# Head of a two-layer encoder kernel: row transfers on ScalarE's queue, the first weight chunk ahead of them, table rows behind the first modulated input

## The reference

```
cond = silu(c)
for i in (0, 1):
    mod = (cond @ mod_w[i] + mod_b[i]).reshape(B, 6, D_MODEL)
    h = modulate(rmsnorm(x, g[0]), mod[:, 0], mod[:, 1])
    y = diff_attention(h, ...)   if i == 0 else   mlstm_layer(h, ...)
    x = x + mod[:, 2][:, None, :] * rmsnorm(y, g[1])
    h = modulate(rmsnorm(x, g[2]), mod[:, 3], mod[:, 4])
    y = swiglu(h, ...)           if i == 0 else   moe_swiglu(h, ...)
    x = x + mod[:, 5][:, None, :] * rmsnorm(y, g[3])
```

## Time and profile before

| what | us |
| --- | --- |
| median of 3 runs | 1612.39 |
| lowest, highest | 1611.19, 1613.15 |
| the profiled execution's own time | 1613.23 |
| span of the profiled execution | 1611.4 |
| TensorE busy in the span | 1493.7 (93%) |
| VectorE busy | 472.5 (29%) |
| ScalarE busy | 161.5 (10%) |
| mean granted clock of TensorE, of full | 0.973 |

### The profile page before, as it was taken

The page is one execution under the profiler, slowest core; times in us unless marked ns, Lnnn a source line. Parts: engine busy times, 40 slices in busy tenths (PEclk is TensorE's granted clock), DMA queues, the critical chain, the costliest instruction groups (busy, mean ns, idle before and its releaser), DMA issues.

```text
span 1611.4 us, 21780 instructions
## 1 busy us (share of the span) xinstructions
PE 1493.7 (93%) x9526; PEld 1091.1 (68%) x9526; DVE 472.5 (29%) x1003; ACT 161.5 (10%) x428; POOL 37.6 (2%) x84
## 2 busy tenths in 40 slices
PE   4997999999999899989999999999898899998997
PEld 3864587885477677443356887778683597886884
DVE  1577327351047455151211111111112311011113
ACT  2005210000020121021000000000000000000000
POOL 1000100000011100010000000000000000000000
PEclk8999999999999999999989999999999999999998
DMA  9996129859432110759998999999999999999995
GB/s 336 387 393 230 57 93 366 320 188 360 156 105 105 53 52 1 274 196 357 401 370 337 392 395 392 395 393 395 393 382 398 389 378 395 392 395 392 395 392 202
DMA packets 205824, 483.49 MB, mean 300 GB/s; under 512 B 4241, under 2 KB 6698, under 8 KB 205714
## 3 DMA queue, kind: packets, MB, share of 16 engines
q1 hardware_dynamic: 205106, 481.46, 79.9%
q10 hardware_dynamic: 608, 0.47, 0.1%
HBM read 480.86 MB, written 1.05 MB: 299 GB/s over the span
## 4 chain that ended last, share of the span: by engine, by line
PE 74%; DMA 13%; DVE 5%; SPq 4%; issue 3%; ACT 1%; POOL 0%; DVEq 0%; POOLq 0%
PE ps L1209 18%; PE ps L1729 15%; PE ps L1196 10%; DMA ring<-in_moe_w_gate 7%; PE ps L1787 7%; PE ps L1745 4%; PE ps L1585 3%; DMA ring<-in_moe_w_down 3%; DMA ring<-in_attn_w_in 3%; SPq L620 2%; PE ps L1752 2%; PE ps L1253 2%; PE ps L1635 2%; PE ps L1797 2%; SPq L617 1%
## 5 line engine op out<-in xcount | busy, mean ns | idle before, releaser
L1209 PE MATMUL ps<-hT,ring 128*128 128x256 f32 x1472 | 326.7, 382 | 5.1 <-issue 1.8
L1209 PEld LDWEIGHTS ps<-hT,ring 128*128 128x128 f32 x1472 | 278.6, 191 | 49.0 <-issue 6.5
L1729 PE MATMUL ps<-arena,ring 128*128 128x208 f32 (+1 forms) x1792 | 295.7, 327 | 6.7 <-DMA ring<-in_moe_w_gate 6.7
L1729 PEld LDWEIGHTS ps<-arena,ring 128*128 128x128 f32 x1792 | 292.8, 191 | 9.5 <-DMA ring<-in_moe_w_gate 9.0
L1196 PE MATMUL ps<-ring,arena 128*128 128x512 f32 x368 | 158.8, 592 | 1.3 <-DVE arena L2243 1.3
L1787 PE MATMUL ps<-arena,ring 128*128 128x208 f32 (+1 forms) x896 | 149.3, 327 | 2.6 <-DMA ring<-in_moe_w_down 2.6
L1787 PEld LDWEIGHTS ps<-arena,ring 128*128 128x128 f32 x896 | 145.2, 190 | 3.7 <-DMA ring<-in_moe_w_down 3.0
L1745 PE MATMUL ps<-ring,arena 128*32 128x256 f32 x1792 | 110.2, 401 | 30.6 <-issue 30.6
L1196 PEld LDWEIGHTS ps<-ring,arena 128*128 128x128 f32 x368 | 69.5, 190 | 87.2 <-issue 87.2
L1745 PEld LDWEIGHTS ps<-ring,arena 128*32 128x32 f32 x1792 | 62.7, 116 | 76.2 <-issue 46.1
L2034 DVE SCALAR_TENSOR_TENSOR arena<-ring,cond,arena 128x512 f32<-128x512 f32 x140 | 105.3, 752 | 5.0
(11 more groups left out here) (348 smaller groups left out, 1089.5 us busy)
## 6 DMA issues: line engine op xcount, KB each, us to landing
ring<-in_moe_w_down SPq DMA_DIRECT2D x56, 2048.0 KB, 19.3
ring<-in_moe_w_gate SPq DMA_DIRECT2D x55, 2048.0 KB, 19.4
ring<-in_moe_w_up SPq DMA_DIRECT2D x55, 2048.0 KB, 20.0
ring<-in_mod_w SPq DMA_DIRECT2D x24, 2048.0 KB, 17.0
ring<-in_mlstm_w_in SPq DMA_DIRECT2D x8, 2048.0 KB, 9.1
ring<-in_attn_w_in SPq DMA_DIRECT2D x6, 2048.0 KB, 19.9
ring<-in_ffn_w_gate SPq DMA_DIRECT2D x5, 2048.0 KB, 12.4
ring<-in_ffn_w_up SPq DMA_DIRECT2D x5, 2048.0 KB, 12.8
```

Of the source, the lines that this page charges most:

```text
L1209: ins = pe.matmul(dst, w[:, k, c * P:(c + 1) * P], hT[:, k, :], start=(k == 0), stop=(k == KT - 1))
L1729: ins = pe.matmul(dst, weights_in[:, k, ft * P:(ft + 1) * P], xq[:, k, BASE:BASE + w], start=(k == 0), stop=(k == KT - 1))
```

## The change

- `sp_program`: behind the wait for `rows_clear` and the transfer of `c`, the first chunk of `mod_w` is issued at once, then `x`, then the other chunks.
- ScalarE waits for `rows_clear` at its start and issues the seven other row transfers.
- Lambda's rows and the seven table transfers are issued by ScalarE behind its part of `hT`.
- TensorE: four products of `keep_busy` ahead of each of the three later `mod_product`s, three behind the first `mod_turn`; `turn_tables` behind j = 1 instead of ahead of j = 0; `spread_gates(0)` and `(1)` behind j = 2 and 3 instead of 0 and 1.
- VectorE: lambda's product behind the copies of j = 1, its rest behind those of j = 3; `fold_gates(0)` and `(1)` behind j = 2 and 3.

```diff
         def sp_program(sp):
             sp.wait_ge(rows_clear, 1)
             sp.dma_start(rows[0:8, 1, :], a["c"][0].rearrange("(t p) -> t p", p=P)).then_inc(rows_loaded, 16)
-            sp.dma_start(rows[8:72, 1, :], a["norm_g"]...).then_inc(rows_loaded, 16)
...
-            sp.dma_start(rows[96:112, 0, :], a["mlstm_norm"][0]...).then_inc(rows_loaded, 16)
-            sp.dma_start(x[:], a["x"][0].rearrange("(t p) d -> p t d", p=P)).then_inc(x_loaded, 16)
             for i, (m, f, n, r) in enumerate(PLAN):
...
                 sp.dma_start(dst, weights(m, f, n)).then_inc(landed[i % SLOTS], 16)
+                if i == 0:
+                    sp.dma_start(x[:], a["x"][0].rearrange("(t p) d -> p t d", p=P)).then_inc(x_loaded, 16)
...
         def act_program(act):
-            act.dma_start(lam_in[:], a["attn_lambda"][0]...).then_inc(lam_loaded, 16)
+            act.wait_ge(rows_clear, 1)
+            act.dma_start(rows[8:72, 1, :], a["norm_g"]...).then_inc(rows_loaded, 16)
...
+            act.dma_start(rows[96:112, 0, :], a["mlstm_norm"][0]...).then_inc(rows_loaded, 16)
...
-            for m, name in enumerate(("mlstm_w_q", "mlstm_w_k", "mlstm_w_v")):
...
-            act.dma_start(b_router[:], ...).then_inc(small_loaded, 16)
             act.wait_ge(consts, 1)
             act.wait_ge(u_free, 1)
...
                 ins.then_inc(u_free, 1)
+            act.dma_start(lam_in[:], a["attn_lambda"][0]...).then_inc(lam_loaded, 16)
+            for m, name in enumerate(("mlstm_w_q", "mlstm_w_k", "mlstm_w_v")):
...
+            act.dma_start(b_router[:], ...).then_inc(small_loaded, 16)
             act.wait_ge(tables_turned, 3)
...
             for j in range(1, EARLY):
+                keep_busy(ps[:, 5], 4)
                 mod_product(0, j, j)
             mods = EARLY
             mod_turn(1)
-            turn_tables()
+            keep_busy(ps[:, 5], 3)
...
-                if j < 2:
-                    spread_gates(j)
+                if j == 1:
+                    turn_tables()
+                elif 2 <= j < 4:
+                    spread_gates(j - 2)
                 if j:
                     for m in MODS[0][j - 1]:
...
-            dve.wait_ge(lam_loaded, 16)
-            link(dve.tensor_tensor(lam_in[:, 0:4:2], ...))
-            dve.tensor_reduce(lam_s, ...).then_inc(lam_ready, 1)
...
-                if j == 0:
+                if j == 1:
+                    dve.wait_ge(lam_loaded, 16)
+                    link(dve.tensor_tensor(lam_in[:, 0:4:2], ...))
+                    dve.tensor_reduce(lam_s, ...).then_inc(lam_ready, 1)
+                if j == 3:
                     dve.wait_ge(lam_ready, 2)
...
-                if j < 2:
+                if 2 <= j < 4:
                     dve.wait_ge(tables_ready, 1)
-                    fold_gates(j)
+                    fold_gates(j - 2)
```

More of the change, by code:

```diff
@@ L624, in sp_program @@
             sp.wait_ge(rows_clear, 1)
-            cw = a["mlstm_conv_w"][0]
             sp.dma_start(rows[0:8, 1, :], a["c"][0].rearrange("(t p) -> t p", p=P)).then_inc(rows_loaded, 16)
[L627 to L633, removed]
-            sp.dma_start(x[:], a["x"][0].rearrange("(t p) d -> p t d", p=P)).then_inc(x_loaded, 16)
             for i, (m, f, n, r) in enumerate(PLAN):
@@ L754, in link @@
                 act.wait_ge(astep, steps.next())
-            act.dma_start(lam_in[:], a["attn_lambda"][0].unsqueeze(0).broadcast_to([P, 4, DA])).then_inc(lam_loaded, 16)
+            act.wait_ge(rows_clear, 1)
+            cw = a["mlstm_conv_w"][0]
+            act.dma_start(rows[8:72, 1, :], a["norm_g"].rearrange("l i (t p) -> (l i t) p", p=P)).then_inc(rows_loaded, 16)
+            act.dma_start(rows[72:73, 1, :], a["attn_subln"]).then_inc(rows_loaded, 16)
+            act.dma_start(rows[0:96, 2, :], a["mod_b"].rearrange("l (t p) -> (l t) p", p=P)).then_inc(rows_loaded, 16)
+            act.dma_start(rows[0:64, 0, :], cw.rearrange("j (t p) -> (j t) p", p=P)).then_inc(rows_loaded, 16)
+            act.dma_start(rows[64:80, 0, :], a["mlstm_conv_b"][0].rearrange("(t p) -> t p", p=P)).then_inc(rows_loaded, 16)
+            act.dma_start(rows[80:96, 0, :], a["mlstm_skip"][0].rearrange("(t p) -> t p", p=P)).then_inc(rows_loaded, 16)
+            act.dma_start(rows[96:112, 0, :], a["mlstm_norm"][0].rearrange("(t p) -> t p", p=P)).then_inc(rows_loaded, 16)
             def normed_x(t):
@@ L822, in act_program @@
                 ins.then_inc(u_free, 1)
+            act.dma_start(lam_in[:], a["attn_lambda"][0].unsqueeze(0).broadcast_to([P, 4, DA])).then_inc(lam_loaded, 16)
+            for m, name in enumerate(("mlstm_w_q", "mlstm_w_k", "mlstm_w_v")):
+                act.dma_start(block_rows[IT * m:IT * (m + 1)],
+                              a[name][0].rearrange("(t g) i o -> t (g i o)", g=P // 4)).then_inc(tables_loaded, 16)
+            act.dma_start(table_rows[0:3 * IT], a["mlstm_w_gate"][0].rearrange("(k p) n -> k (p n)", p=P)).then_inc(tables_loaded, 16)
+            act.dma_start(router_rows[0:KT], a["moe_w_router"][0].rearrange("(k p) n -> k (p n)", p=P)).then_inc(tables_loaded, 16)
+            act.dma_start(b_gates[:], a["mlstm_b_gate"].broadcast_to([P, 2 * MH])).then_inc(small_loaded, 16)
+            act.dma_start(b_router[:], a["moe_b_router"].broadcast_to([P, E])).then_inc(small_loaded, 16)
             act.wait_ge(tables_turned, 3)
@@ L1223, in spread_gates, with keep_busy @@
                               w_gates.rearrange("p k n -> p (k n)"), start=True, stop=True).then_inc(spread_full, 1)
+            def keep_busy(dst, products):
+                for _ in range(products):
+                    pe.matmul(dst[:, 0:3 * P], ident[:], vecs[:], start=True, stop=True)
             pe.wait_ge(consts, 1)
@@ L1289, in values @@
                 pe.matmul(b[:, P:2 * P], aT[:, h % 2, 2 * P:3 * P], v_nat[:, 1, w], start=False, stop=True).then_inc(o_full, 1)
-            def keep_busy(dst, products):
-                for _ in range(products):
-                    pe.matmul(dst[:, 0:3 * P], ident[:], vecs[:], start=True, stop=True)
             scores(0)
@@ L2182, in dve_program @@
                     emptied(ins)
-                if j == 0:
+                if j == 1:
+                    dve.wait_ge(lam_loaded, 16)
+                    link(dve.tensor_tensor(lam_in[:, 0:4:2], lam_in[:, 0:4:2], lam_in[:, 1:4:2], ALU.mult))
+                    dve.tensor_reduce(lam_s, lam_in[:, 0:4:2], AX_X, ALU.add).then_inc(lam_ready, 1)
+                if j == 3:
                     dve.wait_ge(lam_ready, 2)
```

2 lines of the change are left out of this document (removed).

## The result

| | before | changed |
| --- | --- | --- |
| median of 5 runs, us | 1612.48 | 1620.36 |
| lowest, highest | 1611.19, 1613.73 | 1618.11, 1621.74 |
| the profiled execution's own time | 1613.23 | 1618.11 |
| its span | 1611.4 | 1616.4 |
| start of j = 4 | 102.2 | 105.3 |

The ratio is 1.0045 (95%: 1.0034 to 1.0056): **slower by 7.9 us**, where 1612.2 in a range up to 1617 was forecast. The profile of the changed kernel is of its fastest execution, so it holds 4.9 of the 7.9 us.

The account below looks back on a forecast made before the run. TensorE has 74% of the chain; transfers pay only in the first 140 us, judged by j = 4's start. Stream gain 3.6 - 0.7 - 1.6 = 1.3 us, less 1.1 for a spread, leaves 0.2: 1612.2 us, range 1609.5 to 1617.

Parts of the forecast that it names:

- Term 1 and 2: Head of SP's queue: bulk data starts 3.6 us earlier; row transfers sharing with the stream lose 0.7 us (0.3 to 1.2).
- Term 3: Lambda's rows and tables, issued near 36 us into a full stream, cost it 1.6 us (1.2 to 2.0).
- What I cost at nothing: Turned tables behind j = 1 have 1.4 to 3.0 us of cover before j = 2's data; fill products land in waits.
- VectorE: Lambda's product and folds move later at no cost; the fold behind j = 2 keeps 1.8 us of cover.
- Term 4: TensorE's moved gate spreads: behind j = 3 the 1.1 us is paid in full; behind j = 2 it just fits.
- The fills: New fill products, 1.9 us per four and 1.5 per three, buy nothing: 1.7 us saved in j = 0 meets a wait.
- ScalarE's issues wait behind SP's: Small issues on ScalarE held 5.25 us each at the head, rows and perhaps tables late: 1620 to 1626 us; chance 0.12.
- The early products turn late: Half clock in the early products makes hT 6 us late, 2 to 4 beyond cover: 1614.5 to 1616.5; chance 0.09.
- Nothing given back: Small transfers slip into the stream free and the spread hides, so all 3.6 us stay: 1608.8; chance 0.09.

Follow-up runs that it names:

- The second set's profile: The whole changed kernel measured again, against the kernel before: 1616.65 us against 1612.61, ratio 1.0031.
- the third set: The kernel before with only four fill products added ahead of each of the three later early products: 1612.69 us, ratio 0.9999.
- The order alone: The kernel before with only the change's order on TensorE and VectorE, no fills: 1615.07 us (1.0013), on another chip 1614.72 (1.0016).
- its variant with later biases: The changed kernel with the two bias transfers issued behind lambda's exponential: 1617.3 us, ratio 1.0035 to the kernel before.
- the fourth measurement of the changed kernel: The unaltered changed kernel as reference on one chip, against the kernel before: 1617.68 us against 1612.69, ratio 1.0032.
- the version of the third set: The changed kernel with column chunks one place sooner in the plan: 1610.88 us (0.9989), again 1612.09 (0.9998), against the kernel before.
- the third: The unaltered changed kernel on another occasion, against the kernel before: 1621.27 us against 1613.68, ratio 1.0047.
- the head alone: The kernel before with only the change's queue head, row transfers on ScalarE behind lambda's rows and tables: 1612.02 us, ratio 0.9994.

## Why the prediction was wrong, point by point

*Term 1 and 2, the head: right.* 3.6 less 0.7 is 2.9 us; the queues show 3.0 us at 36 us. j = 0 started at 36.54 (36.1 was forecast).

*Term 3, lambda and tables: right kind, mis-sized.* 1.6 us with a bound of 2.0; the stream fell back by 2.9 us. 0.47 MB displaced 1.12 MB, 2.4 times its bytes. The small transfers' own engine time was close to what the earlier trace rows gave (17.0% of 12 us is 2.04 us, for 1.97). But that was no upper bound on what the stream loses: SP's packets took longer beside them, 98 ns of engine time each for 87 (88.9% of 12 us on 16 engines over 1736 packets, against 104.5% over 2302). The chunk of j = 2 was issued 0.4 us sooner than before. That alone would have changed the forecast by 1.3 us, to about 1.1 us lost.

*"What I cost at nothing": this is the step that failed.* It put j = 0 at 36.1 and two times 14.0 behind it, as if j = 1 could start when j = 0 ends, and so found 1.4 to 3.0 us of cover for the turned tables. The chunk of j = 1 was issued 3.3 us sooner (31.81 for 35.12) and landed at 54.73, only 0.3 us sooner than the 55.0 of the third set: between its issue and its landing the stream fell back by the 2.9 us of term 3. j = 1 thus starts 4.7 us later than the 50.1 that the forecast implies, and by terms 1 to 3 themselves, from 55.0, it could not have started before 52.1 to 53.7. At full clock (the second set's profile) it runs from 54.66 to 68.7, and behind it come the turn, two sums and j = 2 at 71.70. No wait for the chunk of j = 2 shows there. From there every moved product is paid: turn 2.5 and spreads 2.6, less the spread that stood behind j = 1 (1.2) and the wait ahead of j = 3 (1.4) that are gone, 2.5 us in all. The order alone, with the transfers of before, shows the same loss: j = 4 2.35 us later, medians 2.1 and 2.0 us higher. The whole change starts j = 1 1.0 us sooner than before and so loses 1.3 us at j = 4 where the clock stays full (103.46), and 3.1 to 6.3 where it doesn't. The failed step by itself makes about 1614.5 us, which the range still held, and the one profiled execution of the changed kernel with full clock took 1614.61. What carries the others towards 1617 and past it are two things that the forecast had at nothing: the clock behind the wait, and a place in the MoE stage (both below).

*VectorE* was costed at nothing, and the chain bears it out: no piece of it stands there from j = 1 to j = 4.

*Term 4, the spreads:* behind j = 3 it is paid, as forecast (1.29 for 1.1). Behind j = 2 it was to fit ahead of j = 3's chunk. It took the place of the wait there: from the start of j = 2 to that of j = 3 it is 15.87 us for 16.04 before. But j = 2 itself was 3.3 us later than my 70.2 (1.5 at full clock), so nothing waits for data at j = 3 any more.

*The fills:* "they buy nothing" was too mild. They also cost more than I took from the earlier trace rows, since one such product is two of its records: four took 2.75 to 2.85 us for my 1.9, and three 2.10 for 1.5. That delayed the last early product by 1.1 us (31.35 for 30.24 without fills), which its shorter run made up. They shorten j = 0 by 1.5 us (2.9 against the second profile without them) and give it to the wait ahead of j = 1 (3.0 to 5.0 us in the profiles with fills and such a wait, 1.9 and 2.5 in the two without fills). Behind that wait the clock was at half in four of the five profiles of the changed kernel and its variant with later biases, at a price of 1.7 to 3.0 us in j = 1 and up to 1.4 in j = 2. Without fills it was so in one of two. The length of the wait doesn't sort these cases: the clock fell behind 1.89 us and stayed full behind 3.91. On one chip the kernel with fills had a median 2.4 us above the one without (1617.68 against 1615.25). Those two intervals overlap, but over all measurements it is 1.0031 to 1.0047 with fills against 1.0018 and 1.0021 without; that the fills cost time is likely and not shown. Where there is no wait (third set) j = 4 starts 2.9 us earlier in the profile with fills (98.21 for 101.09).

*The rivals.* "ScalarE's issues wait behind SP's" named 1620, near the measured time, and its mechanism is refuted: ScalarE's issues took 0.34 to 0.68 us while SP's took 11.66 for three, the rows landed at 10.72, and j = 0 started early, not late. That its number came near is luck. The Trainium skill ("DMA: Bandwidth & Descriptors", Queues, rings and completion order) says that neither queue has a generator of its own; no held issue followed from that here. What the same section says of taking turns fits the trace, which doesn't show the turns themselves: the small transfers got through, and the last row came 5.9 us behind its issue where it was 3.3 us in the emptier head. "The early products turn late" didn't happen: the clock was 1.00 there, and the product of the last early chunk started at 31.35. "Nothing given back" fell with term 3.

*What I did not have as a case:* that the stage behind the wait is where the clock falls. I priced the clock only in the early products and in j = 0.

*From j = 4 to the end.* I held that everything behind j = 4 keeps its spacing. The profiled execution's own time less the start of j = 4 is 1509.7 to 1511.5 us in 14 of the 18 profiles, and 1512.4 to 1513.6 in four. One place that differs is a change of expert group in the MoE stage. Before, the chain there:

```profile
1272.24 5.69 issue
1277.93 5.27 PE ps L1745 x64
```

in the fourth measurement of the changed kernel:

```profile
1277.42 6.69 issue
1284.12 6.50 PE ps L1750 x64
```

and in the second:

```profile
1272.29 6.58 issue
1278.87 4.95 PE ps L1750 x64
```

Two things have to be kept apart. The pause, in which TensorE waits for nothing that the profile shows, goes with the kernel: it is 6.56 to 6.72 us in all eight profiles of kernels that have both the fills and the moved order, and 5.63 to 5.69 in all ten that lack one of them. What differs between executions of one kernel is the products behind it: 4.92 to 4.95 us in four of the eight profiles (for 5.27 to 5.37 behind the shorter pause) and 6.50 to 6.58 in the other four, which are the four above: three of the four of the changed kernel and one of the two of the version of the third set. There the clock is at half for longer: by the stretches of 2 us it is 0.50, 0.50 and 0.52 from 1284 to 1290 in the fourth measurement, and before it was back at 0.69 in the second 2 us of those products.

**The sum of the profiled execution**, own time 4.9 us above before's: j = 1 starts 1.0 sooner; half clock in j = 1 adds 1.8, the turn in place of a spread 1.2, the spread behind j = 3 1.3, and the spread in place of the wait ahead of j = 3 takes off 0.2. So j = 4 starts 3.1 later. The group change adds 2.3 (6.72 and 6.56 us for 5.69 and 5.27), and with 0.5 less elsewhere it is 4.9. A slower execution (1620.79) has 6.3 of it at j = 4 and 1.3 behind it.

**What stays open.** The changed kernel's medians lay 7.9, 4.0, 7.6 and 5.0 us above before. The fall of the clock (5.0 us at j = 4 between two executions of the same kernel) and the products behind the group change (1.6 us) have the size of that spread. What decides in an execution how long the clock stays low was not found, and nor was what makes the pause 1 us longer in the kernels with both fills and moved order; neither was tried by itself. The last three measurements were made on three different chips, and the five executions of the third lie within 1.8 us at 1620.3 to 1622.0, so a part played by the chip isn't ruled out.

## What to carry to other kernels

A start without idle time in a trace is no slack: work out when each piece of data lands (issue and latency) even where nothing waits for it, since here 0.7 us hid the one chunk that bounds the stage. Moving small transfers about in a full stream gained nothing here: each way of placing all of them left SP's queue at 15.88 to 15.94 MB by 48 us, while the order of the large chunks against the work that needs them moved the start of j = 4 by 7 us with the rest of the change, and by 0.6 us in the kernel before. Small work that fits ahead of a data wait is free, behind the last one it is not; and what products that keep an engine busy give can be swallowed by the next wait.

## What the hardware showed that I had not expected

- 0.47 MB in 608 packets on a second queue beside a full stream displaced 1.12 MB of it; with 288 of the packets, 0.01 MB between them, moved elsewhere it displaced 0.02 MB less.
- Two engines issue side by side: one is held for 11.66 us over three issues, the other's take 0.34 to 0.68 us each. The longest beside a held queue was 1.37 us, once, with the head alone.
- The same kernel, with the same wait of 3 to 5 us ahead of the same 64 products, had them at 14.08, 15.77, 17.04 and 17.09 us in four profiles.
- A pause of TensorE some 1170 us behind the edit was 6.56 to 6.72 us long in the eight profiles of kernels with both parts of it, and 5.63 to 5.69 in the ten others.
